# Preparation of a recurrence spread over four engines, six gate tiles computed inside the sampled tokens' attention, and low parts made tile by tile

## The reference, cut to what matters

```python
h = rmsnorm(x, attn_norm)
z = h @ w_in                       # [RWKV-7 columns | attention columns | 2 x 1024 merge gates]
# RWKV-7, prepared for all tokens, then a recurrence over them
w = -softplus(-(w0 + tanh(wl) @ w_up)) - 0.5;  a = sigmoid(a0 + al @ a_up);  g = sigmoid(gl) @ g_up
kk = k * k_k / max(norm(k * k_k), 1e-12);      k = k * (1 + (a - 1) * k_a)
decay = exp(-exp(w));  bonus = sum(r * k * r_k) * v
merged = sigmoid(zg[:, :1024]) * (o_r @ w_rwkv_out) + sigmoid(zg[:, 1024:]) * (o_n @ w_nsa_out)
x = x + merged @ w_out             # then an expert layer and a gated per-layer embedding, not touched here
```

## Time and profile before

| | |
|---|---|
| three runs | 2902.58, 2902.8 and 2910.75 us, median 2902.8 |
| profiled execution, span from first to last instruction | 2903.8 us (its own time is not given apart from the span) |
| busy share | PE 88%, PEld 75%, DVE 50%, ACT 35%, POOL 31% |
| mean granted TensorE clock | 0.93 of full speed |
| stages, from the timeline | projection 21.8 to 193.9; preparation to 278.3; recurrence to 499; prompt attention 700 to 816.8; sampled attention to 917.3; gate projection to 1031.4; merge to 1107.1; the rest is untouched |

### The profile page before, as it was taken

One profiled execution on the slowest core, in us unless ns is written; L12 is line 12 of the kernel. 1 busy time (PEld: TensorE's weight loads), 2 busy tenths in 40 slices (PEclk: granted clock), 3 DMA queues, 4 the chain that ended last, 5 costly groups with the idle time before them and its releaser, 6 DMA issues. The chain is left out here.

```text
span 2903.8 us, 51463 instructions
## 1 busy us (share of the span) xinstructions
PE 2569.2 (88%) x20574; PEld 2165.9 (75%) x20574; DVE 1443.5 (50%) x3149; ACT 1030.4 (35%) x1819; POOL 896.8 (31%) x782
## 2 busy tenths in 40 slices
PE   7984887898866998799999988799999999999969
PEld 6973885686545978799999877667777777677748
DVE  3354444314744224479999855344444444444443
ACT  2012111223622020134444466444444444444432
POOL 0000000000000000001111555577777777777710
PEclk9986997897976999899999999899999999999989
DMA  3210000522212220156656444899999999999932
GB/s 118 81 34 21 4 4 18 184 83 69 64 35 66 66 88 30 58 176 186 184 183 186 144 173 173 294 344 349 337 336 344 345 350 337 335 346 358 342 129 69
DMA packets 206886, 511.22 MB, mean 176 GB/s; under 512 B 31938, under 2 KB 99010, under 8 KB 205186
## 3 DMA queue, kind: packets, MB, share of 16 engines
q1 hardware_dynamic: 150338, 340.04, 34.8%
q0 software_dynamic: 56320, 167.98, 16.0%
HBM read 463.49 MB, written 48.56 MB: 176 GB/s over the span
## 5 line engine op out<-in xcount | busy, mean ns | idle before, releaser
L2335 POOL TENSOR_TENSOR wide<-wide,sif 128x2048 f32<-128x2048 f32 (+1 forms) x10 | 52.7, 5267 | 1580.8 <-DVE wide L2451 1580.8
L2585 POOL DMA_INDIRECT dots<-dots,place x320 | 373.7, 1168 | 125.8 <-issue 97.2
L2589 POOL DMA_INDIRECT v_row<-in_peer_v,expert x320 | 367.0, 1147 | 97.5 <-issue 97.5
L2720 DVE TENSOR_TENSOR v_lo<-v_raw,v_hi 128x1024 fp32r<-128x1024 f32 x128 | 157.1, 1227 | 367.9 <-ACT v_hi L2669 367.9
L2200 PE MATMUL ps<-h_hi,u_hi 128*128 128x320 f32 x1024 | 321.5, 314 | 10.7 <-DVE u_lo L2357 10.7
L2200 PE MATMUL ps<-h_lo,u_hi 128*128 128x320 f32 x1024 | 317.5, 310 | 0.0
L2200 PE MATMUL ps<-h_hi,u_lo 128*128 128x320 f32 x1024 | 317.4, 310 | 0.0
L2611 PE MATMUL ps<-h_hi,u_hi 128*128 128x256 f32 x1024 | 300.6, 294 | 11.5 <-DVE u_lo L2715 11.5
L2611 PE MATMUL ps<-h_lo,u_hi 128*128 128x256 f32 x1024 | 292.4, 286 | 0.0
L2611 PE MATMUL ps<-h_hi,u_lo 128*128 128x256 f32 x1024 | 292.2, 285 | 0.0
L2611 PEld LDWEIGHTS ps<-h_hi,u_hi 128*128 128x128 f32 x1024 | 197.8, 193 | 87.0 <-issue 70.2
(11 more groups left out here) (489 smaller groups left out, 5257.9 us busy)
## 6 DMA issues: line engine op xcount, KB each, us to landing
u_raw<-in_peer_u SPq DMA_DIRECT2D x256, 512.0 KB
v_raw<-in_peer_v SPq DMA_DIRECT2D x128, 512.0 KB
dots<-dots SPq DMA_DIRECT2D x128, 160.0 KB, 1.8
g<-gate_matrix SPq DMA_DIRECT2D x32, 512.0 KB, 8.0
wt<-in_w_in SPq DMA_DIRECT2D x24, 512.0 KB, 3.6
pages<-in_cmp_pages SPq DMA_DIRECT2D x64, 128.0 KB, 2.0
kv_pages<-in_sel_pages SPq DMA_DIRECT2D x64, 128.0 KB, 2.0
wt<-in_w_zg SPq DMA_DIRECT2D x16, 512.0 KB, 3.6
```

What stands on the lines that cost most here:

```text
L2335: nc.gpsimd.tensor_tensor(hot4, hot4, which, ALU.mult).then_inc(numbered, 1)
L2585: nc.gpsimd.indirect_dma_start(dots[:, s:s + 1], None, dots_flat, bass.IndirectOffsetOnAxis(f.place[:, s:s + 1], 0)).then_inc(d_got[s % SL ...
L2589: nc.gpsimd.indirect_dma_start(v_row(s), None, v_rows, bass.IndirectOffsetOnAxis(f.expert[:, s:s + 1], 0)).then_inc(v_got[s % SLOTS], 16)
L2720: nc.vector.tensor_tensor(v_lo[:, j % 2], v_raw[:, j % RV], v_hi[:, j % 2].bitcast(F32), ALU.subtract).then_inc(v_parted, 1)
```

## The change

- **Preparation.** The steps become counters by tile. TensorE makes 21 products, each into one of three pairs of banks (`pair`), and starts one when the reader of the pair has taken it. The square of the keys and two of the last four multiplications go to GpSimd (`r.ht` and `r.rt`). `r.ht`'s products with `r_k` have a buffer of their own (`prods`). `up`, `keep`, `masks` and `ident2` are loaded during the first projection (`early`), and the last two are no longer loaded in the recurrence.
- **Gates.** The first projection writes the scaled x into `k.x` itself. `SideTiles` computes gate tiles 10 to 15 in `sample_attention_stage` from that x with float32 operands as they are, in 12 units (`make`, a unit is half a tile: eight calls of 288 columns), all into bank 4; ScalarE copies each unit out (`take`), and a unit waits until the one before is copied. The gate projection has 10 tiles, with no scaling. The original x is loaded again during the merge.
- **Merge.** `m_lo` of tile n-1 is made right behind tile n.

```diff
-                project_stage(k, ring, 2 * KD, "attn_norm", h, k.zg)
+                project_stage(k, ring, GATE_MAIN, "attn_norm", h, k.zg, place="made")
...
+    def make(self, pe, u, bank, c0=0, c1=KD):
+        t, h = u // 2, u % 2
+        if c0 == 0:
+            pe.wait_ge(self.arrived[t % self.SIZE], 16 * (t // self.SIZE + 1))
+            if u:
+                pe.wait_ge(self.taken, u)
+        wt = self.slots[t % self.SIZE].rearrange("p (c n) -> p c n", n=P)
+        for c in range(c0, c1):
+            mm = self.k.nc.tensor.matmul(self.k.bank(bank, TH), wt[:, c, :], self.k.x[:, c, h * TH:(h + 1) * TH],
+                                         start=c == 0, stop=c == KD - 1)
+        if c1 == KD:
+            mm.then_inc(self.made, 1)
...
+        side_within = {0: 4, 1: 5, 2: 8, 3: 10}
+        side_after = {1: (6, 7), 3: (11,)}
+        side_before = {3: (9,)}
...
             scores(0)
+            side.make(pe, 1, SIDE_BANK)
             importance(0)
+            side.make(pe, 2, SIDE_BANK)
+            side.make(pe, 3, SIDE_BANK)
             for g in range(NG):
                 if g + 1 < NG:
                     scores(g + 1)
+                for u in side_before.get(g, ()):
+                    side.make(pe, u, SIDE_BANK)
                 turn_past(g)
+                side.make(pe, side_within[g], SIDE_BANK, 0, 4)
                 if g + 1 < NG:
                     importance(g + 1)
-                turn_rest_and_mix(g)
+                turn_rest(g)
+                side.make(pe, side_within[g], SIDE_BANK, 4, 8)
+                mix_all(g)
+                for u in side_after.get(g, ()):
+                    side.make(pe, u, SIDE_BANK)
...
+        @block.gpsimd
+        def _(pool):
+            pool.wait_ge(keyed, 1)
+            nc.gpsimd.tensor_tensor(tmp, kk[:], kk[:], ALU.mult).then_inc(squared, 1)
+            pool.wait_ge(prodded, 4)
+            pool.wait_ge(raised, 2)
+            nc.gpsimd.tensor_tensor(r.ht, r.ht, cum, ALU.mult).then_inc(mixed, 1)
+            nc.gpsimd.tensor_tensor(r.rt, r.rt, tmp, ALU.mult).then_inc(mixed, 1)
+            pool.wait_ge(mixed, 2)
...
+            act.wait_ge(differed, 1)
+            nc.scalar.activation(tmp, cum, ACT.Exp, scale=-DECAY).then_inc(raised, 1)
+            act.wait_ge(raised, 1)
+            nc.scalar.activation(cum, cum, ACT.Exp, scale=DECAY).then_inc(raised, 1)
+            nc.scalar.activation(sw, sw, ACT.Exp, scale=-DECAY).then_inc(raised, 1)
...
+            for n in range(4):
+                product(W + n, up[0:64, 0, n * P:(n + 1) * P], xs[0:64, 12, :])
+            for n in range(4):
+                product(A + n, up[64:128, 0, n * P:(n + 1) * P], xs[64:128, 12, :])
+            pe.wait_ge(squared, 1)
...
+            for n in range(4):
+                product(G + n, up[:, 1, n * P:(n + 1) * P], xs[:, 13, :])
+            for n in range(4):
+                pe.wait_ge(prodded, n + 1)
+                product(BONUS + n, k.blocks[:], prods[:, n, :])
+            pe.wait_ge(inverted, 1)
+            for n in range(4):
+                product(UNIT + n, k.spread[:, n, :], norms[:])
...
-            for n in range(KD):
-                dve.wait_ge(rounded, n + 1)
-                last = nc.vector.tensor_tensor(m_lo[:, n, :], out[:, n, :], m_hi[:, n, :].bitcast(F32), ALU.subtract)
-            ch.link(last)
+                if n:
+                    low(n - 1)
+            ch.link(low(KD - 1))
```

More of the change, by code:

```diff
@@ L285, in scale @@
     def scale(self, dve, c):
-        if c >= 3:
+        if self.place == "made":
+            return
+        if c >= 3 and self.place == "ring":
             dve.wait_ge(self.lowered, c - 2)
-        self.k.nc.vector.scalar_tensor_tensor(out=self.own[:, c % 3, :], in0=self.k.x[:, c, :], scalar=self.k.par(self.gain, c),
+        self.k.nc.vector.scalar_tensor_tensor(out=self.own(c), in0=self.k.x[:, c, :], scalar=self.k.par(self.gain, c),
                                               in1=self.k.rs[:], op0=ALU.mult, op1=ALU.mult).then_inc(self.normed, 1)
@@ L299, in rest, with __init__, load, take @@
                                        ALU.subtract).then_inc(self.lowered, 1)
-def project_stage(k, weights, ntiles, gain, rhs, dst, gates=None, shift=None):
+class SideTiles:
+    SIZE = 3
+    def __init__(self, k, ctx, w, first, count, slots, outs):
+        self.k, self.w, self.first, self.count, self.slots, self.outs = k, w, first, count, slots, outs
+        self.arrived = k.sems(ctx, *[f"side_in{b}" for b in range(self.SIZE)])
+        self.made, self.taken = k.sems(ctx, "side_made", "side_taken")
+    def load(self, sp, t):
+        if t >= self.SIZE:
+            sp.wait_ge(self.made, 2 * (t - self.SIZE) + 2)
+        sp.dma_start(self.slots[t % self.SIZE], self.w[self.first + t]).then_inc(self.arrived[t % self.SIZE], 16)
+    def make(self, pe, u, bank, c0=0, c1=KD):
[10 more added lines that the diff above has]
+            mm.then_inc(self.made, 1)
+    def take(self, act, u, bank):
+        t, h = u // 2, u % 2
+        act.wait_ge(self.made, u + 1)
+        self.k.nc.scalar.activation(self.outs[t][:, h * TH:(h + 1) * TH], self.k.bank(bank, TH), ACT.Copy).then_inc(self.taken, 1)
@@ L306, in project_stage @@
+def project_stage(k, weights, ntiles, gain, rhs, dst, gates=None, shift=None, early=(), place="ring"):
     nc = k.nc
@@ L527, in _ @@
-            last.then_inc(v_at, 1)
-            dve.wait_ge(e_at, E.at("bonussum"))
-            for n in range(4):
-                last = nc.vector.tensor_tensor(halves(r.bonus[:, n, :]), k.pair(2 * n), halves(xs[:, 8 + n, :]), ALU.mult)
-            last.then_inc(v_at, 1)
-            dve.wait_ge(s_at, S.at("decays"))
+                dve.wait_ge(made, BONUS + n + 1)
+                nc.vector.tensor_tensor(halves(r.bonus[:, n, :]), k.pair(pair(BONUS + n)), halves(xs[:, 8 + n, :]),
+                                        ALU.mult).then_inc(dve_took, 1)
@@ new lines, in _ @@
+            nc.scalar.activation(xs[:, 13, :], xs[:, 13, :], ACT.Sigmoid).then_inc(low, 1)
+            act.wait_ge(kept9, 1)
+            for first, dst, bias in ((W, sw, "w0"), (A, r.bt, "a0")):
+                for n in range(4):
+                    act.wait_ge(made, first + n + 1)
+                    nc.scalar.activation(halves(dst[:, n, :]), k.pair(pair(first + n)), ACT.Sigmoid,
+                                         bias=k.par(bias, n)).then_inc(act_took, 1)
+            act.wait_ge(made, SUM + 1)
@@ new lines, in product @@
+            def product(i, lhs, rhs):
+                begin(i)
+                for h in range(2):
+                    mm = nc.tensor.matmul(k.bank(pair(i) + h, TH), lhs, rhs[:, h * TH:(h + 1) * TH], start=True, stop=True)
+                mm.then_inc(made, 1)
+            pe.wait_ge(r.early_in, 16 * len(r.early))
+            pe.wait_ge(low, 1)
+            for n in range(4):
+                product(W + n, up[0:64, 0, n * P:(n + 1) * P], xs[0:64, 12, :])
+            for n in range(4):
+                product(A + n, up[64:128, 0, n * P:(n + 1) * P], xs[64:128, 12, :])
@@ L1830, in _ @@
                 sp.dma_start(dst, k.d[name]).then_inc(loaded, 16)
+            for t in range(1, 5):
+                side.load(sp, t)
             for g in range(cached.SLOTS, NG):
@@ L1833, in _ @@
                 cached.load(sp, g)
+            side.load(sp, 5)
         @block.tensor
         def _(pe):
+            side.make(pe, 0, SIDE_BANK)
             pe.wait_ge(loaded, 16 * len(tables))
@@ L2063, in _, with low @@
             ch = Chain(dve, chain)
+            def low(n):
+                dve.wait_ge(rounded, n + 1)
+                return nc.vector.tensor_tensor(m_lo[:, n, :], out(n), m_hi[:, n, :].bitcast(F32), ALU.subtract)
             for n in range(KD):
```

228 lines of the change are left out of this document (121 added, 107 removed).

## The result

Five executions of the changed kernel took 2805.9 to 2827.41 us, median 2809.56, against 2902.8 before: ratio 0.9675, 95% interval [0.9645, 0.9705]. I forecast 2838, range 2825 to 2853. The execution that was profiled is the slowest of the five (2827.41).

A forecast was written before the change was run, and what follows sets the result against it. TensorE idles in preparation (no engine bounds it) and sampled attention, but paces the gate projection; 2903.8 - 30.3 (preparation) - 2.9 (recurrence) + 10.5 (sampled attention) - 38.4 (gates) - 3.8 (merge), less 1.0, gives 2838 us, range 2825 to 2853.

The forecast's parts named there:

- the failed step: Sampled attention: gate units overrun the idle gaps, some starting cold; 10.5 us lost.
- If the clock stayed high through, it would be 7: Sampled attention: with TensorE's clock high throughout, the gate units would lose 7 us instead of 10.5.
- step 1: Preparation: TensorE's eight w and a products over 64 rows, all at half clock, take 16.1 us, to 212.6.
- the rival that had the clock rise: Preparation: clock rises inside the 64-row products, about 10.5 instead of 16.1 us, total 2831; chance 0.22 with the port rival.
- Step 2: Preparation: GpSimd's square takes 5.2 us, is done near 204 before TensorE wants it, and costs nothing.
- Step 3: Preparation: TensorE's sum of squares and g, 5 us at half clock, then faster: 10.5 us, to 223.1.
- Step 4: Preparation: ScalarE copies the last g tile, loads the table and makes two exponentials, ending at 229.2.
- Step 5: Preparation: GpSimd's two and VectorE's three last passes exclude each other, ending at 247.3; stage gain 30.3 us.
- Recurrence, gates and merge: Gains of 2.9 us (no wait for masks and ident2), 38.4 (six gate tiles less) and 3.8 (seven low parts moved).
- dearer units: Sampled attention: cold starts or a cold clock make the gate units cost 22 instead of 10.5 us, total 2850; chance 0.17.
- arriving late weights: Gate projection: lost cover of x scaling reappears as another wait, 10 us, total 2848; chance 0.04.
- units wholly exposed: Sampled attention: all 12 gate units on the path at half clock cost 101 us, total 2929, slower than before; chance 0.02.

The follow-up runs named there:

- gates_back: Changed kernel with no gate units in the sampled attention and all 16 tiles back in the gate projection: 2861.09 us, ratio 0.9851.
- one_call: Changed kernel with the eight calls of every gate unit cut to one (two in units cut in halves): 2819.22 us, ratio 0.9705.
- half_units: Changed kernel with each gate unit making four of its eight calls: 2801.86 us, ratio 0.9662.
- again: Changed kernel run and profiled a second time, nothing edited: 2813.15 us, ratio 0.9687, profiled span 2814.5 us.
- rt_first: Changed kernel with GpSimd's last two multiplications swapped, r.rt ahead of r.ht: 2808.2 us, ratio 0.9674.
- best: Changed kernel with w and a products in turn, four pairs of banks, and r.rt ahead of r.ht on GpSimd: 2804.5 us, ratio 0.9658.

## Why the prediction was right in sign and wrong in size

**Sampled attention: the failed step.** "Sum: 4.4 - 1.3 + 0.9 + 6.8 = 10.8, say 10.5 us lost" is where 16.8 of the 24.4 us between forecast and the second profile's span lie, and more than all of the 13.3 to the first's. I counted the units as guests in gaps whose clock was given: cold behind each mixing (units 6, 7, 9 and 11), a little warmth returned to the next scores. The units change the clock of the whole stage. TensorE is now busy 85.59 of 94.1 us at clock 1.00; without the units' 50 us that leaves some 36 for the stage's own rows, which took 60.82 before. The scores and the mixing, at half clock before, nearly halve. So group 0's mixing ends 35.2 us into the stage, where I had it 1.4 later than the old 39.8, and group 3's scores start at 61.4 and not at about 68. The case "If the clock stayed high through, it would be 7" had the right condition and the wrong price: it left the old rows at their old durations. One row that tells it stood in the prediction's own group: the turning, at 1.53 and at 2.82 in one stage. The trace before has the mixing and the page product at their slow durations alone (3.04 to 3.63, and 3.64 to 3.67), so their price at full clock had to be inferred from the turning. With `gates_back`, `one_call` and `half_units` the cause is shown.

**Preparation, step 1.** 16.1 us for the eight products was too much in every profile: the first product of `a` overlapped the last of `w` (13.94 even at 0.50 throughout), and in six of nine profiles the clock rose inside them (11.5 to 11.7). There the rival that had the clock rise was right in kind; I had taken 8.05 us at 0.50 as proof for 16. In the other three, the first profile among them, it was not: the clock rose only in the 128-row work behind. The rule named beside the rival (the Trainium skill, "TensorE: Matmul & The Clock Gate", section "What's actually happening", by which activity releases the throttle) agrees with the six; in the three, 13.7 to 13.9 us of products without a pause did not raise the clock.

**Step 2** stands, with a detail: GpSimd's square took 4.03 and not 5.2, and it does hold VectorE (the first scan lasts 2.99, the last 1.33), but ScalarE's next tiles pace the scans anyway (the last scan follows the last `w` tile at once).

**Step 3** had 10.5 and measured 9.4 (210.07 to 219.5): the clock rose 3.1 us into that work, and I had taken 5. **Step 4** stands: 6.3 us from TensorE's end to the second exponential's, where I had 6.1.

**Step 5** stands: the passes exclude each other. They ended 3.8 us earlier than I had, and 3.5 of that comes from steps 1 and 3. The limit that I put beside it, that VectorE with at most one SBUF input is not held, left out a condition that the same section of the Trainium skill ("SBUF — State Buffer", "Who interferes with whom") gives with it: outside the 2-port perf modes, in which VectorE works through both of its SBUF ports. The products from PSUM kept their 0.76; the copy of 0.2 us did not. And I summed five durations without asking which pass gets the port first. In the changed kernel the order costs 2.5 us against VectorE alone, in "again" it gains 1.7, and `rt_first` shows another 2.1 for two swapped lines.

**Recurrence, gates and merge** were right: 2.9 and 3.6 for 2.9 (the same recurrence took 212.7 to 218.3 in thirteen profiles, so what shows the 2.9 is that VectorE's first copy no longer waits, and not the stage's length); 37.8 and 36.8 for 38.4; 3.9 and 2.8 for 3.8. The gate projection gives a little back at its start: the first matmul stands 6.5 us behind the last unit's copy where it stood 6.0 behind the stage's end.

**The range** took its lower end from the port and the clock of the preparation and 3.5 us from the sampled attention. It had no case in which the sampled attention became shorter. One with the old rows at full clock, at the 16.8 us that this measured, moves the sum from 2838 to 2821, and the lower end with it. The rivals with dearer units, arriving late weights or units wholly exposed did not come true; their chances, 0.23 together, belonged on the other side.

## What to carry to other kernels

Work put into a stage whose engine idles is not priced by the gaps alone: if TensorE's clock is at its lower level there, price the stage's own matmuls again at the higher one, and if one row stands there at both durations, it gives the ratio. Half of the added rows raised the clock nearly as far as all of them here; beyond that, only covered rows are free. Then look for a stretch that no clock shortens: here the 26 us up to the pages of group 3, in which added rows cost nothing.

Between VectorE and GpSimd, ask for each GpSimd pass which VectorE instruction it will lie beside. Beside products from PSUM it was free, beside passes of two SBUF inputs the two run one after the other, and the order decides whether it helps or hurts.

## What the runs showed of the hardware that I had not expected

- A small strided copy with a single SBUF input was held by GpSimd as long as a large pass: 4.90 us where it takes 0.19. A RECIPROCAL with a single SBUF input was not: it took its usual 3.75 wholly inside a GpSimd pass (216.99 in `best`). My rule of "at most one SBUF input" was too simple. The Trainium skill, "SBUF — State Buffer", section "Who interferes with whom", lists copies among the instructions that can use both ports, when their operands meet its conditions, and then contend; the copy's row agrees.
- Two products over 64 rows each, on the lower and the upper partitions, ran beside each other on TensorE: 2.29 us for both where one takes 1.92, at half clock. The Trainium skill, "TensorE: Matmul & The Clock Gate", section "Part 3: Packing small matmuls — row/col tiling", says that such products overlap; the runs agree, and show what it asks of the program: enough banks (12.1 us with three pairs, all at half clock, and 6.99 with four, the last 1.6 at the higher level).
- In the same program TensorE's clock rose 9 us after the first product in some executions and 17 in others, and 3.5 us of the preparation hang on it.
- The experts' block, which nothing here touches, took 948.5 to 960.1 us in thirteen profiles of changed kernels, and so moves a single execution by more than most edits above.
